# Both first units of two feed-forward entries multiplied together, and what goes with it

## The reference

```python
mod = (cond @ ada_w[l] + ada_b[l])[:, None, :]
sh_m, sc_m, g_m, sh_f, sc_f, g_f = jnp.split(mod, 6, axis=-1)
...
x = layer_norm(DN_ALPHA * x + (1.0 + g_m) * y, ln_mix_g[l], ln_mix_b[l])
h = x * (1.0 + sc_f) + sh_f
u = causal_dwconv(h @ w_up, conv_w)      # w_up 1024 x 5632, three taps
val, gate = u[..., :D_FF], u[..., D_FF:] # D_FF = 2816
y = (jax.nn.silu(gate) * val) @ w_down
```

## Time and profile before

| what | us |
|---|---|
| median of 3 runs | 1171.91 (1170.33 to 1173.24) |
| the profiled execution | 1170.72 |
| its span, first to last instruction | 1168.9 |
| PE busy in the span | 1119.3 |
| POOL, ACT, DVE busy | 830.8, 590.7, 539.7 |
| entry one in the trace: first transpose to third unit | 172.97 to 193.60 |
| entry two: the same | 476.00 to 496.86 |

### The profile page before, as it was taken

How to read it: one execution, slowest core, us unless ns; L and a number is a source line. 1 busy time by engine, 2 the same in 40 slices (tenths; PEclk the granted TensorE clock), 3 DMA queues, 4 the chain that set the end, 5 groups by cost and what they waited for, 6 DMA issues and landing times.

```text
span 1168.9 us, 21669 instructions
## 1 busy us (share of the span) xinstructions
PE 1119.3 (96%) x8115; PEld 1026.5 (88%) x8115; DVE 539.7 (46%) x1120; ACT 590.7 (51%) x894; POOL 830.8 (71%) x295
## 2 busy tenths in 40 slices
PE   5899999999999989999999999999999999999997
PEld 1799898999998988999999868999999988999996
DVE  4568877766567674693323451343111333111112
ACT  0455525455453564555545444565876543544444
POOL 3477569988876636799787747556566776988884
PEclk9899999999999999899999999999999999999999
DMA  9986798999987445596656416444444645666652
GB/s 325 320 285 184 247 297 272 337 321 330 301 291 230 127 133 181 177 296 215 203 168 196 128 46 187 129 144 138 128 133 145 197 145 149 210 183 191 184 182 87
DMA packets 253484, 238.03 MB, mean 204 GB/s; under 512 B 18075, under 2 KB 216528, under 8 KB 253424
## 3 DMA queue, kind: packets, MB, share of 16 engines
q1 hardware_dynamic: 235104, 198.70, 55.1%
q10 hardware_dynamic: 17712, 38.28, 9.1%
q0 software_dynamic: 608, 0.22, 0.1%
HBM read 236.12 MB, written 1.05 MB: 203 GB/s over the span
## 4 chain that ended last, share of the span: by engine, by line
PE 61%; POOL 13%; issue 8%; ACT 6%; DVE 6%; DMA 5%; SPq 0%; POOLq 0%; ACTq 0%; DVEq 0%
PE bank L1294 14%; PE bank L1295 13%; PE bank L1296 13%; POOL unit_lo L733 4%; POOL unit_lo L792 4%; POOL down L795 4%; ACT unit_hi L855 2%; PE bank L1328 2%; PE bank L1319 2%; PE bank L1320 2%; DMA raw<-in_ev_w_in 2%; PE bank L1355 1%; DMA raw<-in_w_in 1%; PE bank L1348 1%; PE bank L1349 1%
## 5 line engine op out<-in xcount | busy, mean ns | idle before, releaser
L733 POOL TENSOR_TENSOR unit_lo<-raw,unit_hi 128x2048 fp32r<-128x2048 f32 (+5 forms) x87 | 343.8, 3957 | 215.9 <-ACT unit_hi L855 215.0
L1294 PE MATMUL bank<-h_hi,unit_hi 128*128 128x256 f32 x1152 | 326.8, 284 | 0.0
L1295 PE MATMUL bank<-h_lo,unit_hi 128*128 128x256 f32 x1152 | 325.9, 283 | 0.0
L1296 PE MATMUL bank<-h_hi,unit_lo 128*128 128x256 f32 x1152 | 325.9, 283 | 0.0
L792 POOL TENSOR_TENSOR unit_lo<-raw,unit_hi 128x2048 fp32r<-128x2048 f32 (+1 forms) x70 | 257.2, 3674 | 71.7 <-ACT unit_hi L1006 66.0
L1294 PEld LDWEIGHTS bank<-h_hi,unit_hi 128*128 128x128 f32 x1152 | 220.7, 192 | 4.9 <-issue 2.1
L1295 PEld LDWEIGHTS bank<-h_lo,unit_hi 128*128 128x128 f32 x1152 | 220.8, 192 | 2.5
L1296 PEld LDWEIGHTS bank<-h_hi,unit_lo 128*128 128x128 f32 x1152 | 220.8, 192 | 0.0
L855 ACT ACTIVATE unit_hi<-raw 128x2048 fp32r<-128x2048 f32 (+5 forms) x97 | 161.2, 1664 | 97.0 <-PE bank L1296 30.4
L795 POOL TENSOR_TENSOR down<-raw_down,down 128x1024 fp32r<-128x1024 f32 x70 | 176.2, 2517 | 0.3 <-ACT down L1032 0.3
L2199 DVE SCALAR_TENSOR_TENSOR work<-bank,cols,work 128x254 f32<-128x254 f32 (+1 forms) x176 | 72.6, 474 | 128.4 <-ACT work L993 128.4
(11 more groups left out here) (365 smaller groups left out, 2172.3 us busy)
## 6 DMA issues: line engine op xcount, KB each, us to landing
raw<-in_ffn_w_up SPq DMA_DIRECT2D x86, 512.0 KB, 5.2
raw<-in_w_in SPq DMA_DIRECT2D x60, 512.0 KB, 4.6
raw_down<-in_ffn_w_down SPq DMA_DIRECT2D x44, 512.0 KB, 5.4
ada<-in_ada_w ACTq DMA_DIRECT2D x16, 1024.0 KB, 7.0
raw<-in_w_up SPq DMA_DIRECT2D x64, 256.0 KB, 3.1
raw_down<-in_w_down SPq DMA_DIRECT2D x32, 512.0 KB, 3.5
raw<-in_ev_w_in SPq DMA_DIRECT2D x28, 512.0 KB, 5.2
att<-in_ada_w ACTq DMA_DIRECT2D x14, 1024.0 KB, 8.0
```

Of the source, the lines that this page charges most:

```text
L733: nc.gpsimd.tensor_tensor(ul[g % 2][:, w], raw_home(g)[:, w], uh[g % 2][:, w].bitcast(F32), ALU.subtract).then_inc(lo_up, 1)
L1294: nc.tensor.matmul(o, sh, mh, start=first, stop=False)
L1295: nc.tensor.matmul(o, sh, ml, start=False, stop=False)
L1296: return nc.tensor.matmul(o, sl, mh, start=False, stop=last)
```

## The change

At both entries PE multiplies the first two units together (`first_pair`): per slice of h four matmuls of the first unit (high and low weights) and two of the second (high weights), then `h_lo` for the first unit, then the second unit's low weights, then `h_lo` for the second. The number of matmuls is the same, 96 for the two units. POOL makes the second unit's low half ahead of `h_low`, behind a wait: at entry one for the normalised rows, at entry two for the modulation columns. ACT loads the Silu table ahead of block 0's scaling, with an activation of one column. In block 0 of both feed-forwards ACT copies the third unit's high half (`hi_unit(g0 + 2)`) behind `y_hi` and no longer ahead of the Silu. The high copy of the first down rows goes behind all of `h_hi` at entry one. DVE makes modulation sum 13 ahead of the first residual and the other two between the residuals; the modulation columns come ahead of the normalisation. ACT issues the transfer for sum 15 one unit earlier.

```diff
@@ POOL, entry one; entry two is alike, behind evacuated(pool, ("modc", 1, 1)) @@
             powers(("even",), spread, LN_EPS)
+            pool.wait_ge(row_ready, 2)
+            lo_unit(G_EO[-1] + 2)
             h_low(1)
             lo_down(FFN_D0[0])
-            lo_unit(G_EO[-1] + 2)
             ffn(0)
@@ ACT @@
-                    if (n, q) == (1, 1):
-                        hi_down(FFN_D0[0])
...
+                    first = fixed and half and b == 0
+                    if first:
+                        nc.scalar.activation(table_scratch, cond[:, 0:1], ACT.Silu)
                     act.wait_ge(bank_full[4 + s], i + ((g0 + k) // 2 + 1))
...
-                    if last:
+                    if last or first:
                         pass
                     elif fixed:
                         hi_unit(g0 + b + 2)
...
                     elif fixed:
+                        if first:
+                            hi_unit(g0 + 2)
                         hi_down(d0 + b + 1)
...
                 other(g)
-                if j == 1:
+                if j == 0:
                     load_sum(SUM_EVEN[2])
             h_high(1, ("modc", 0, 1), modT[:, 0, 24:32], modT[:, 0, 16:24])
+            hi_down(FFN_D0[0])
@@ PE @@
+            def first_pair(n, g):
...
+                for kt in range(KD):
+                    pe.wait_ge(h_hi, highs(n, kt))
+                    for i in range(2):
+                        multiply(g, i, kt, uh, hh, start=kt == 0 and i == 0)
+                        multiply(g, i, kt, ul, hh)
+                    if kt == 0:
+                        unit_begin(g + 1)
+                    for i in range(2):
+                        multiply(g + 1, i, kt, uh, hh, start=kt == 0 and i == 0)
+                for kt in range(KD):
+                    h_low_ready(n, kt)
+                    for i in range(2):
+                        close(g, i, kt, uh, hl)
+                pe.wait_ge(lo_up, g + 2)
+                for kt in range(KD):
+                    for i in range(2):
+                        multiply(g + 1, i, kt, ul, hh)
+                for kt in range(KD):
+                    for i in range(2):
+                        close(g + 1, i, kt, uh, hl)
...
-                    first_units((1, 3)[f], [g0])
-                    second_unit(g0 + 1)
+                    first_pair((1, 3)[f], g0)
@@ DVE, entry one @@
-            mixer_residual(G_EO, 0, ("last", 0), lambda j: [modulation_half(a, bank[7][:, :]) for a in SUM_EVEN[j:min(j + 1, 2)]],
-                           lambda tt: modulation_part(SUM_EVEN[2], bank[7][:, :], (2 * tt, 2 * tt + 1)))
+            modulation_half(SUM_EVEN[0], bank[7][:, :])
+            mixer_residual(G_EO, 0, ("last", 0), lambda j: [modulation_half(a, bank[7][:, :]) for a in SUM_EVEN[1:][j:j + 1]])
+            mod_columns(0, (1,), (0, 0))
             normalize_rows(("even",), 0)
-            mod_columns(0, (1,), (0, 0))
```

More of the change, by code:

```diff
@@ L825, in _ @@
             both_powers(("odd",), LN_EPS)
+            evacuated(pool, ("modc", 1, 1))
+            lo_unit(G_OO[-1] + 2)
             h_low(3)
             lo_down(FFN_D0[1])
-            lo_unit(G_OO[-1] + 2)
             ffn(1)
@@ L1465, in first_units, with multiply, close @@
                                 final(part, mm)
+            def first_pair(n, g):
+                unit_begin(g)
+                pe.wait_ge(lo_up, g + 1)
+                def multiply(u, i, kt, weight, h, start=False, stop=False):
+                    a = slot(u) + kt * UC + P * i
+                    return nc.tensor.matmul(bank[4 + u % 2][:, S * i:S * (i + 1)], weight[u % 2][:, a:a + P], h[:, kt, :],
+                                            start=start, stop=stop)
+                def close(u, i, kt, weight, h):
+                    mm = multiply(u, i, kt, weight, h, stop=(kt, i) == (KD - 1, 1))
+                    if (kt, i) == (KD - 1, 1):
+                        mm.then_inc(bank_full[4 + u % 2], 1)
+                for kt in range(KD):
[18 more added lines that the diff above has]
+                        close(g + 1, i, kt, uh, hl)
             def transpose_rows(n, src, ready=None):
```

## The result

The changed kernel takes 1176.55 us (median of 6 runs, 1175.60 to 1177.22), the kernel before 1170.73 in the same series (1168.61 to 1173.24): a ratio of 1.0049, 95% interval 1.0035 to 1.0064. It is slower, by half a per cent. The profiled execution took 1175.6, its span is 1173.8, against 1168.9.

A forecast was written before the change was run, and what follows sets the result against it. PE was taken as the bound, busy 1119 of 1169 us. Terms 1.6 + 2.0 + 0.75 + 1.1 - 0.55 = +4.9 on 1170.72 gave 1175.6, on the median 1176.8; range 1171.5 to 1181.5.

The forecast's parts named there:

- The core: At each entry, PE's old 1.84 us stop at the second unit is exchanged for stops of 1.0 and 3.1 us.
- the port: DVE's restoring pass and POOL's third low half exclude one another at the entries: 0 or +1.1 us each, taken once.
- the clock: PE's clock at the entries: late rise 0 to +1.5 us, taken +0.75; fall in new idle stretch, taken 0.
- Second unit's low half at no cost: Entry one: POOL makes it early, h_lo ends about 183.6 as PE needs it; cost 0 to 0.2 us, taken 0.
- Pairing: Both first units together: 16 second-unit matmuls come before the first unit is complete, which is 1.92 us later.
- The chain behind te: From PE's first matmul after the first unit completes: product, y_hi, copy, POOL; third unit at +10.7 us instead of +10.61.
- Rival 1: Faster: third low half and y_lo in time, third unit at te+6.6, together -4.6 us, 1167.3; chance 0.10.
- Transposes 0.9 later: Entry one: DVE makes the columns ahead of normalisation, so PE's transposes start about 173.85 instead of 172.97 us.
- Rival 3: Much slower: DVE first at both entries, clock falls in both idle stretches or rises late; +8.8 us, 1180.7; chance 0.17.
- y_lo waits: Two PE waits in first feed-forward blocks four and five can vanish: 0 to -1.1 us, taken -0.55.
- entry one +2.30: Forecast for the first entry: first unit's completion +1.5 us, third unit's start another 0.1, together +1.6.
- entry two +1.16: Forecast for the second entry: first unit's completion +1.92 us, third unit's start another 0.1, together +2.0.

The follow-up runs named there:

- copy back: Changed kernel with the third unit's high copy again ahead of the Silu: 1169.56 us, ratio 0.9983 to the kernel before.
- table late: Changed kernel with the third unit's high copy again ahead of the Silu and without the early table load: 1171.34 us, ratio 1.0014.
- DVE back: Changed kernel with entry one's modulation sums, their load and the order of normalisation and columns as before: 1179.66 us, ratio 1.0071.
- pair only: Kernel before with only PE's and POOL's edits and the moved first down copy; ACT's block 0 and DVE as before: 1171.53 us, ratio 1.0022.
- ACT alone: Kernel before with only ACT's early table load and the third unit's high copy behind y_hi: 1171.87 us, ratio 1.0003.
- changed a, b and c: Three traces of the unaltered changed kernel; executions of 1175.6, 1178.54 and 1175.59 us.

## Why the prediction was right, and where it was not

The time (1176.8 forecast, 1176.55 measured) and the sum of +4.9 on the profiled execution are right. The median moved by more, 5.8 (from 1170.73); the forecast counted from 1171.91, the median of the first three runs, which was 1.2 too high, and so that the two times agree to 0.25 is partly luck. The core is right by its steps; the terms for the port and the clock are not, and they offset one another.

- **Second unit's low half at no cost.** Right: POOL's copy runs 174.87 to 179.44, `h_lo` until 183.66 (183.6 forecast), and PE passes from `h_lo` to the low weights at te without a stop.
- **Pairing.** The first transpose to te is 0.95 longer at entry one and 1.07 at entry two, where a shorter low clock is in it. Forecast for entry one was +1.92 - 0.9, less 0.4 if the clock rose at the same moment. It did (177.2, before 177.3), so 0.6 stands against 0.95. The working has a slip: eight matmuls at 0.21 and 40 at 0.12 are 6.5, not 6.6, which leaves 1.1 for the short waits.
- **The chain behind te.** Down product at te+4.81 (4.85 forecast), wait 0.80 (1.0). Copy at te+4.03 (4.1), POOL until te+10.6, third unit te+10.71 and +10.70 (+10.7), stops 2.89 and 2.93 (3.1). These stops, and the low clock behind one of them, are the changed kernel's loss; copy back takes them away and ends below the kernel before. Rival 1's condition, a copy ahead of te+1.0, is met there (te+0.93), and its mechanism holds: but the third unit came at te+7.66, not +6.6, since that rival took `y_lo` to be in time, and the wait for it (0.80) is still there; it also left out that the first feed-forward takes back part of the gain (182.27, before 181.65).
- **Transposes 0.9 later.** They are 1.25 later. Behind PE's last column sum they start 1.76 later; 1.65 was forecast, or 1.5 by the addends (172.2 + 0.7 + 0.8 is 173.7, not 173.85). What I missed is the load for sum 15, issued at 151.7 (before 157.4), while the transfer of unit 18's weights is under way. That transfer, issued at 148.8, takes 9.35 (before 6.99), ACT waits 5.83 for the unit at 158.25 (before 3.85 for PE), and PE 1.07 for its low half (the L1382 wait above). The part ahead of it was 1.07 earlier than before, so it barely shows in the sum. The wait is there (0.8 to 1.2), with a transfer of 9.1 to 9.4, in four of the nine traces of kernels with the earlier load and in none of the five without, where the transfer takes 6.9 to 8.0; the load was not tested by itself.
- **The port (+1.1 taken).** It did not come. POOL was first at both entries, by 0.05, and DVE's pass paid (5.58); so it was in all three traces of this kernel. I had read 4.10 in the earlier trace rows as the pass's own length; in table late, where it starts 0.15 ahead of the end of POOL's copy, it takes 1.23. What POOL pays for this pass falls on the next down rows' low half, 3.4 instead of 2.4, in every kernel here, the one before too, and PE does not wait for it. Where this lock does reach PE is on the columns (DVE back, pair only), and the forecast did not see that.
- **The clock (+0.75 for the rise, 0 for the fall).** Wrong both ways. At entry one the low stretch is as before (173.8 to 177.2, before 173.9 to 177.3), at entry two it is shorter (477.6 to 481.0, before 474.3 to 481.1). The fall behind the stop, priced at 0 because stops of 1.84 did no harm, cost 2.5 in the second feed-forward. Rival 3 had it with 3.0 for both entries.
- **y_lo waits (-0.55).** Right in kind, mis-sized: 1.6 became 0.3, and the stage is 1.22 shorter. In copy back, where PE is early, one wait alone is 1.6 and the stage 0.62 longer than before. So it isn't a gain of the change: these blocks take up part of what PE is early or late.

Net: port +1.1 and rise +0.75 were not there (-1.85), the fall was (+2.54), and the `y_lo` waits gave 0.67 more than forecast: +0.02. The other terms missed too: entry one +2.30 (1.6 forecast), entry two +1.16 (2.0), and +0.12 in stages that had none, together -0.02. A right total with wrong terms of this size is partly luck.

## What to carry to other kernels

Moving one engine's work ahead in a chain of four engines exposes what the old order hid: follow the third consumer, not the second; here the stop removed at the second unit (1.84) came back at the third (2.9) because the copy that feeds it had been moved behind the chain's end, and one line put back took the whole loss away, down to 0.17% below the kernel before at best. A stop on PE costs more than its length if the clock falls behind it, so compare the stages behind the stop too, in several traces. Before a long POOL instruction is released early, look for two-input DVE instructions that can be caught behind it, however small.

## What the runs showed of the hardware that was not expected

- An instruction of 128x8 on DVE with two SBUF inputs took 3.75 us behind a POOL copy of 4.52, and 0.16 without it.
- Behind PE stops of 2.9 us the granted clock fell to 0.50 (1.2 GHz) in eight of ten cases, for 3.4 or 6.8 us; behind stops of 2.09 in one of four (pair only, entry two), behind stops of 1.84 in three of 14 near 443 and in none of four at the entries of the kernel before and ACT alone. The same schedule can have it in one execution and not in the next (entry one of changed a, b and c), and each such stage is 1.2 to 2.9 us longer.
- With useless matmuls in the stop the clock stayed up (none of six fell), and the kernel was not faster.
- A DVE or POOL row's length can hold a wait for the other engine: the pass of 128x1024 on DVE has rows of 1.23, 2.55, 4.10 and 5.58 (table late, copy back, before, changed a, entry one), where POOL's copy had 0.15, 1.5, 3.0 and 4.5 left when it started: what was left, and 1.1 of its own.
